# Products that only occupy TensorE between the layers of a two-block transformer, replaced by waiting

## What is computed

```
x = x + conv_glu_ffn(rms_norm(x, g_ffn), ...)        # w_up, w_down
h = rms_norm(x, g_final)                             # seam "final"
h = h + 0.5 * rmsnorm(swiglu(rmsnorm(h, ff1_pre_g), ...), ff1_post_g)    # seam "ff1_post"
z = rmsnorm(h, mix_pre_g) @ w_in
...
h = h + rmsnorm(o @ w_out, mix_post_g)               # seam "mix_post"
h = h + 0.5 * rmsnorm(swiglu(rmsnorm(h, ff2_pre_g), ...), ff2_post_g)    # seam "ff2_post"
gate = sigmoid(rmsnorm(h, ple_pre_g) @ w_ple_gate)
h = h + rmsnorm(gate * (p @ w_ple_proj), ple_post_g)                     # the end, "ple_post"
```

## Time and profile before

| | |
|---|---|
| median of 3 runs | 3308.14 us (3307.93 to 3308.61) |
| the profiled execution, its own time | 3308.55 us |
| its span, first to last instruction | 3306.7 us |
| mean granted clock of TensorE | 0.996 |
| TensorE busy with matmuls | 3250.7 us (98%), 19964 records |
| VectorE busy | 2105.9 us (64%) |
| ScalarE busy | 1587.6 us (48%) |
| `keep_busy`, L552 | 124 records of 128x512: 84 on HR, 28 on T1R, 12 on OPR, median 0.39 us |

### The profile page before, as it was taken

One profiled execution on the slowest core, in us unless ns is written; L12 is line 12 of the kernel. 1 busy time (PEld: TensorE's weight loads), 2 busy tenths in 40 slices (PEclk: granted clock), 3 DMA queues, 4 the chain that ended last, 5 costly groups with the idle time before them and its releaser, 6 DMA issues.

```text
span 3306.7 us, 51352 instructions
## 1 busy us (share of the span) xinstructions
PE 3250.7 (98%) x19964; PEld 2889.8 (87%) x19964; DVE 2105.9 (64%) x2263; ACT 1587.6 (48%) x1903; POOL 97.5 (3%) x39
## 2 busy tenths in 40 slices
PE   8999999999999999999999999999899999999997
PEld 7999988888888888888888887998888888888886
DVE  6676677666665547656555547766886556555577
ACT  5445556555444335444444435446544444444355
POOL 0000200000000100000000000000110000000001
PEclk9999999999999999999999999999999999999999
DMA  8555555666665555655665554754456666565553
GB/s 262 175 153 167 189 166 172 191 192 188 185 191 190 188 188 159 197 186 189 184 191 190 188 187 134 223 153 122 141 160 196 185 190 186 182 197 185 191 168 128
DMA packets 321884, 595.78 MB, mean 180 GB/s; under 512 B 18292, under 2 KB 42004, under 8 KB 321748
## 3 DMA queue, kind: packets, MB, share of 16 engines
q1 hardware_dynamic: 313872, 587.27, 56.9%
q10 hardware_dynamic: 7876, 6.63, 0.7%
HBM read 591.70 MB, written 2.13 MB: 180 GB/s over the span
## 4 chain that ended last, share of the span: by engine, by line
PE 95%; DVE 3%; ACT 1%; issue 1%; POOL 0%; DMA 0%; ACTq 0%; DVEq 0%; POOLq 0%
PE acc L616 26%; PE acc L618 25%; PE acc L621 24%; PE acc L656 5%; PE acc L658 5%; PE acc L659 5%; DVE wl L1610 1%; PE acc L552 1%; ACT wh L1071 0%; PE acc L673 0%; DVE HF L2309 0%; PE acc L853 0%; PE acc L854 0%; PE acc L855 0%; PE acc L760 0%
## 5 line engine op out<-in xcount | busy, mean ns | idle before, releaser
L1610 DVE TENSOR_TENSOR wl<-raw,wh 128x1024 fp32r<-128x1024 f32 x1112 | 1385.0, 1255 | 1013.8 <-ACT wh L1071 1012.4
L1071 ACT ACTIVATE wh<-raw 128x1024 fp32r<-128x1024 f32 x1112 | 1165.7, 1057 | 1297.1 <-PE acc L621 1025.0
L618 PEld LDWEIGHTS acc<-OPR,wl 128*128 128x128 f32 x4992 | 940.1, 188 | 207.3
L616 PE MATMUL acc<-OPR,wh 128*128 128x512 f32 x2658 | 1040.5, 397 | 19.2 <-DVE wl L1610 11.8
L618 PE MATMUL acc<-OPR,wl 128*128 128x256 f32 x4992 | 1010.7, 279 | 0.0
L621 PE MATMUL acc<-OPR,wh 128*128 128x512 f32 x2334 | 924.8, 396 | 0.0
L616 PEld LDWEIGHTS acc<-OPR,wh 128*128 128x128 f32 x2658 | 505.2, 190 | 38.4 <-issue 14.3
L618 PEld LDWEIGHTS acc<-HR,wl 128*128 128x128 f32 x2208 | 414.8, 188 | 95.0
L616 PE MATMUL acc<-HR,wh 128*128 128x512 f32 x1138 | 447.1, 396 | 1.0 <-DVE HF L1624 1.0
L618 PE MATMUL acc<-HR,wl 128*128 128x256 f32 x2208 | 439.7, 278 | 0.0
L621 PEld LDWEIGHTS acc<-OPR,wh 128*128 128x128 f32 x2334 | 438.2, 188 | 0.0
(11 more groups left out here) (353 smaller groups left out, 2083.4 us busy)
## 6 DMA issues: line engine op xcount, KB each, us to landing
raw<-in_w_up SPq DMA_DIRECT2D x176, 512.0 KB, 4.4
raw<-in_ff_w_gate SPq DMA_DIRECT2D x176, 512.0 KB, 3.7
raw<-in_ff_w_up SPq DMA_DIRECT2D x176, 512.0 KB, 4.4
raw<-in_ff_w_down SPq DMA_DIRECT2D x176, 512.0 KB, 3.9
raw<-in_w_in SPq DMA_DIRECT2D x170, 512.0 KB, 4.1
raw<-in_w_down SPq DMA_DIRECT2D x88, 512.0 KB, 3.8
raw<-in_w_out SPq DMA_DIRECT2D x64, 512.0 KB, 3.8
raw<-in_w_ple_gate SPq DMA_DIRECT2D x32, 512.0 KB, 3.8
```

Source lines behind the costliest of these rows:

```text
L616: pe.matmul(acc[:, b + t, :], wh[:, s, col:col + P], x, start=first, stop=False)
L618: mm = pe.matmul(acc[:, b + t, 0:T], wl[:, s, col:col + P], x[:, 0, :], start=False, stop=last and t % 2 == 0)
L1071: act.activation(wh[:, s, :], raw[:, s, :], ACT.Copy).then_inc(hi_done, 1)
L1610: dve.tensor_tensor(wl[:, s, :], raw[:, s, :], wh[:, s, :].bitcast(F32), ALU.subtract)\
```

## The change

TensorE's 124 products of `keep_busy` are left out, and the function with them. Where they stood, TensorE goes to its next semaphore wait: in the middle of `post_stat` to the one for the squares, at its end to the one for the square root. Nothing else differs, and the output is the same, since nobody read these products.

```
--- before
+++ after
@@ -545,18 +545,11 @@
             colsum = S[:, 1024:1280]
 
-            def keep_busy(name, n):
-
-                x = T1R[:, 0:2, :] if name == "mix_post" else OPR[:, 0, :, :] if name == "ple_post" else HR[:, 0, :, :]
-                for _ in range(n):
-                    pe.matmul(acc[:, post_bank(name) - 3, :], x[:, 0, 0:P], x, start=True, stop=True)
-
             def post_stat(name):
 
                 pe.wait_ge(colsum_ready, N[name] + 1)
                 pe.wait_ge(acc_free, last_of(PH[UNDER[name]]))
                 pe.matmul(acc[:, post_bank(name), 0:T], ones[:, :], colsum, start=True, stop=False)
-                keep_busy(name, 12 if name == "ple_post" else 8)
                 for h in range(2):
                     pe.wait_ge(post_sq, 2 * POSTS[name] + h + 1)
                     for k in range(2):
@@ -564,8 +557,6 @@
                         mm = pe.matmul(acc[:, post_bank(name), 0:T], ones[:, :], S[:, at:at + T],
                                        start=False, stop=h == 1 and k == 1)
                 mm.then_inc(stat_ready, 1)
-                if name != "ple_post":
-                    keep_busy(name, 20)
                 pe.wait_ge(var_ready, N[name] + 1)
```

More of the change, by code:

```diff
@@ L546, in _ @@
             colsum = S[:, 1024:1280]
[L548 to L552, removed]
             def post_stat(name):
```

## The result

The change makes the kernel slower: 3317.47 us (median of 9 runs, 3314.55 to 3318.62), against 3308.05 us for the kernel before (9 runs, 3307.84 to 3310.59). The ratio, run against run, is 1.0024, with a 95% interval from 1.0016 to 1.0032. By the ratio that is 8 us, by the medians 9.4. I had forecast 3314.5 in a range of 3311.2 to 3317.4: the direction holds and the ratio times 3308.05 gives 3316.0, inside the range, but the median itself lies 0.07 us above its upper end, and the loss is larger than the 6.35 us of my sum.

A forecast was written before the change was run, and what follows sets the result against it. TensorE, busy for 95% of the span, was taken to bound the kernel. The terms -0.3, +5.85 (1.95 for each of three dense GEMMs), 0 for in_c and +0.8 for the stats made +6.35 us: 3314.5 us, range 3311.2 to 3317.4.

The forecast's parts named there:

- The reading of the bound: Whole kernel: TensorE holds 95% of the span; in the long GEMMs a microsecond it loses is one of the kernel.
- The fall in each seam: All four seams: pauses of 4.1 us or more drop the granted clock to 0.50.
- Rival B: All seams: the clock holds and TensorE is only freed 0.3 us earlier, 3307.8 us; chance 0.10.
- The upper end of 5.8 us: Dense GEMMs: longest low-clock stretch inside the GEMM, taken from the kernel's start, a loss of 2.6 us.
- rival C: All four seams: longer low stretches, as at the kernel's start, and in_c pays too, +12.1 us, 3320.2; chance 0.08.
- The 0.45: Dense GEMMs: each microsecond of low clock loses 0.45 us, from periods of 1.28 and 0.70 us.
- rival D: Dense GEMMs: a low-clock microsecond costs a full half, in all +6.95 us, 3315.1; chance 0.06.
- The zero for in_c: Second seam: the clock falls, but TensorE's waits for its operand hold the loss, 0 us.
- The -0.3 us in the first seam: First seam: without the 20 products in its queue, TensorE starts the next GEMM 0.3 us earlier.
- the term of the stat matmuls: First seam, third seam and end: squares slowed by an already low clock, +0.8 us, bounds 0 and 3.5 us.
- rival A: Each seam: the clock falls as summed, +3.75 to +9.1 us, 3311.9 to 3317.2; chance 0.74.
- none below 1.8 us: Pauses in the kernel before: four of 2.41 us or more brought clock falls, while one of 1.77 us did not.

The follow-up runs named there:

- e1: Kernel before without the 20 products behind the squares in each seam, those ahead kept: 3315.0 us against 3308.77, ratio 1.0016.
- e5: Kernel before without the products in the first seam only: 3311.54 us against 3308.84, ratio 1.0008.
- e6: Kernel before without the products in the third seam only: 3312.24 us against 3308.84, ratio 1.0010.
- e7: Kernel before without the products in the fourth seam only: 3311.01 us against 3308.84, ratio 1.0005.
- e10: Kernel before without the 20 products behind the squares in the third seam, the 8 ahead kept: 3310.19 us against 3308.49, ratio 1.0006.
- e3: Kernel before without the products in the second seam only, into in_c: 3308.54 us against 3308.77, ratio 0.9999.
- e2: Kernel before without the 8 products (12 at the end) ahead of the squares, the 20 behind kept: 3312.07 us against 3308.77, ratio 1.0007.
- e4: Kernel before without the 12 products at the end only: 3309.22 us against 3308.77, ratio 1.0000.
- e9: Kernel before without the 8 products ahead of the squares in the third seam, the 20 behind kept: 3309.58 us against 3308.49, ratio 1.0004.
- e12: Kernel before with 18 products for 20 in the first seam, more in two wo_a pauses and 19 in gate_pairs: 3305.01 us against 3308.49, ratio 0.9990.

## Why the prediction was right, and where it was off

*The reading of the bound held.* The long GEMMs behind the first and the third seam have no wait to swallow a loss, and VectorE's lag keeps what it gained there up to the next seam (0.70 us at 1300 and at 2000 in the profile after).

*The fall in each seam held*, which rested on four pauses of the trace before: low behind all four in the profile after and in e1's. Rival B, that the squares keep the clock, has fallen with it. Of each dense GEMM's low stretch the profiles of after, e1, e5, e6, e7 and e10 show ten cases: 3.02, 2.86, 3.24, 4.53, 4.32, 3.41, 5.99, 5.13, 4.28 and 6.20 us. Their mean is 4.3 us, the figure I took; that it comes out so exactly is luck, since the ten reach from 2.86 to 6.20 us. The upper end of 5.8 us was a little low: e5 and e10 pass it, and e10's 6.20 us pass the 6 us that I had named as a sign of rival C. The other half of C, that in_c pays, did not come. (C's reason, that the kernel's start met only sparse work, is not what its rows show: from 12.70 to 15.96 the matmuls stand close together.) With 0.45 us lost per microsecond the term is 1.95 us a seam, and e7, where nothing else is lost, measured +2.2. The 0.45 itself can be checked, stretch by stretch, with VectorE's lag over each dense GEMM's start: 4.28 us low in e7 make 1.93 and the lag grew by 1.92; 6.20 us in e10 make 2.79 and it grew by 2.79; 3.24 us in the fourth seam after the change make 1.46, and it grew by 1.44. By the half of the Trainium skill ("TensorE: Matmul & The Clock Gate", "HAM oscillation — how this bites in real kernels") these would be 2.14, 3.10 and 1.62. The measurement decides for the row, and rival D has fallen: the measured lag lies at 0.45 in all three.

*The zero for in_c held*, e3 and the waits above show it. Rival C had in_c paying and has fallen.

*The -0.3 us in the first seam held*: the first GEMM matmul starts at 1264.56 instead of 1265.29, 0.73 us sooner, of which 0.44 is the lead that the kernel had there already. The lag over the seam grew by 1.14 us, and 3.02 x 0.45 - 0.3 is 1.06.

*The step that was off is the term of the stat matmuls, +0.8 us.* I counted a quarter of its bound of 3.5 us, since "the pauses here are shorter than that second one". The profiles have the places where a pause of 2.4 us or more stands ahead of the squares ten times (three in after, three in e2, one each in e4, e5, e6 and e9), and nine of the ten are slow: 2.40 us becomes 3.0 to 3.7 us. Its price comes out as e9's +1.1 us for the third seam, e4's +0.45 us for the end (0.85 us in the profile after), where the table load covers part, and for the first seam what e5 has beyond the GEMM's term, 2.7 - (1.95 - 0.3) = about 1.0 us. Together 2.5 us instead of 0.8. With it the sum is 5.55 + 2.5 = 8.1 us, and the single places gave 8.5. The medians behind these three figures are not clear of the noise one by one; the lags of the single profiles (0.7 and 1.2 us up to the reciprocal of the first seam in e2 and e5, 0.9 to 1.1 in the third of after, e2, e6 and e9, 0.5 to 0.9 at the end) are of the same size. How the end pays stands in ScalarE's row of the square root, first before, then after: it used to follow its table load at once, and now waits for the squares.

```profile
3291.15 0.47 ACT L1157 ACTIVATE S<-acc,SM 128x256 f32<-128x256 f32 x1
```

```profile
3297.16 0.47 ACT L1148 ACTIVATE S<-acc,SM 128x256 f32<-128x256 f32 x1 [0.86 <-PE acc L557]
```

The upper end of rival A, 9.1 us, took 1.6 us for this term, where its own bound was 3.5, and gave no reason for it. That is part of why the median came to lie at the end of the range.

*The chances.* I gave a slower time by over 0.2% 0.45 and a time within it 0.53. The ratio of 1.0024 is on the slower side; the line lay inside the interval. The profile alone could have moved this: the pause of 2.41 us that was followed by a low clock is as long as those ahead of the squares, and I weighed it for the GEMMs but not for the squares.

## What to carry to other kernels

Where a core waits 2.4 us or more with dense matmuls behind the wait, products of settled operands into a free PSUM bank can pay, for some lines of code: here 2.2 to 3.4 us in a seam ahead of a long GEMM, 1.2 us in gate_pairs and 1.5 us for two pauses of wo_a together. Below 4 us of wait it is an average, since not every execution loses anything; look for such pauses in TensorE's timeline together with the granted clock of the stretches behind them, since the page's row of tenths hardly shows them (9 in every slice before, 9 in all but the last after). They are worth nothing where the work behind waits for another engine anyway, as in in_c. Keep their number a little under the pause: they stand in the queue ahead of the real work, and are themselves slow once the clock has fallen.

## What the runs showed of the hardware

A low clock is not only a matter of the pause behind the stats: pauses of 2.4 to 3.1 us slowed the eight short records that followed in nine cases of ten, while 1.7 us did in none of six. Away from the kernel's start and end, low stretches lasted 3.41 or 6.83 us and once, in the third seam of the profile after, 10.24 us (2431.52 to 2441.76); the kernel before had in its profile only the shortest. The same kernel is so timed differently from one execution to the next: after 1.77 us of idle time at 580 the clock stayed up in the profile before and in eleven others, and was low from 580.18 to 583.59 in that of e5 and from 581.00 to 584.42 in that of e1, and VectorE's lag is 1.6 us larger behind it in each. So the prediction's "none below 1.8 us" held for the one profile that it had. A kernel that fills its pauses, e12, has the narrowest times of all, ten of eleven within 0.9 us.
